# Output projection: drawing the last quarter's sixteen products together and placing the first block's logits, transposes and counts behind them

## The reference

```
h = rmsnorm(x) ;  proj = h @ w_in
merged = sigmoid(g_conv) * y_conv + sigmoid(g_attn) * y_attn
x = x + merged @ w_out                       # the output projection
logits = rmsnorm(x) @ w_router + b_router    # 32 experts
top 4 of 32, gates = softmax of the four
x = x + sum over the four experts of gate * (swiglu(h2 @ w_up[e] + b_up[e]) @ w_down[e] + b_down[e])
```

## Time and profile before

| | |
|---|---|
| three runs | 1146.79, 1147.54, 1148.38 us, median 1147.54 |
| the profiled execution: span from the first to the last instruction | 1145.4 us |
| its own time outside the span | not given by the profile; the median of the runs is 2.1 us over the span |
| PE busy | 1097.6 us (96% of the span) |
| DVE, ACT, POOL busy | 437.5, 188.0, 88.4 us |
| DMA | 444.36 MB, 388 GB/s over the span |
| mean granted TensorE clock | 0.993 |

### The profile page before, as it was taken

How to read it: one execution, slowest core, us unless ns; L and a number is a source line. 1 busy time by engine, 2 the same in 40 slices (tenths; PEclk the granted TensorE clock), 3 DMA queues, 4 the chain that set the end, 5 groups by cost and what they waited for, 6 DMA issues and landing times.

```text
span 1145.4 us, 15065 instructions
## 1 busy us (share of the span) xinstructions
PE 1097.6 (96%) x6055; PEld 497.1 (43%) x6055; DVE 437.5 (38%) x858; ACT 188.0 (16%) x398; POOL 88.4 (8%) x161
## 2 busy tenths in 40 slices
PE   9999999999999999999898999999999999999997
PEld 6689898543333333333333333333333333333332
DVE  4577786753433223233223232323232323232322
ACT  2133341221321101010101010101010101010101
POOL 1785215000000000000000000000000000000000
PEclk9999999999999999999999999999999999999999
DMA  9947629999999999999999999999999999999997
GB/s 313 314 128 186 210 85 353 416 357 425 400 420 426 419 432 431 430 433 431 433 433 429 434 430 433 435 428 434 429 434 431 431 434 429 435 429 434 425 423 287
DMA packets 53206, 444.36 MB, mean 388 GB/s; under 512 B 13101, under 2 KB 19373, under 8 KB 35741
## 3 DMA queue, kind: packets, MB, share of 16 engines
q1 hardware_dynamic: 46712, 435.83, 91.7%
q0 software_dynamic: 5600, 7.32, 2.4%
q10 hardware_dynamic: 852, 0.64, 0.2%
HBM read 439.78 MB, written 2.37 MB: 386 GB/s over the span
## 4 chain that ended last, share of the span: by engine, by line
PE 62%; DMA 37%; DVE 0%; issue 0%; ACT 0%; ACTq 0%; SPq 0%; DVEq 0%
PE pA L2051 32%; PE pB L2051 21%; DMA ring<-in_w_up 21%; DMA ring<-in_w_down 10%; PE pM L2051 6%; DMA area<-in_w_up 5%; PE pM L2054 1%; PE pA L2054 1%; DMA x<-in_x_prompt 1%; ACT area L1269 0%; DVE x L1898 0%; SPq L800 0%; DVE conv_row L1812 0%; DVE area L1973 0%; DVE x L1978 0%
## 5 line engine op out<-in xcount | busy, mean ns | idle before, releaser
L2051 PE MATMUL pA<-ring,hn 128*64 128x512 f32 x1536 | 352.6, 602 | 23.0 <-DMA ring<-in_w_up 23.0
L2051 PEld LDWEIGHTS pA<-ring,hn 128*64 128x64 f32 x1536 | 105.3, 137 | 218.8 <-issue 185.5
L2051 PE MATMUL pB<-ring,area 128*64 128x512 f32 (+2 forms) x784 | 171.5, 591 | 6.6 <-DMA ring<-in_w_down 5.8
L2051 PE MATMUL pA<-area,hn 128*64 128x512 f32 x512 | 119.3, 610 | 10.4 <-DMA area<-in_w_up 10.4
L2051 PE MATMUL pB<-area,ring 128*128 128x132 f32 (+2 forms) x928 | 126.4, 327 | 0.0
L2051 PEld LDWEIGHTS pB<-area,ring 128*128 128x128 f32 (+1 forms) x928 | 106.7, 175 | 18.2 <-issue 2.3
L2051 PEld LDWEIGHTS pB<-ring,area 128*64 128x64 f32 (+2 forms) x784 | 58.5, 136 | 101.2 <-issue 87.8
L1898 DVE TENSOR_TENSOR x<-pM,x 128x512 f32<-128x512 f32 x60 | 40.1, 691 | 147.7 <-PE pM L2051 147.7
L1257 ACT ACTIVATE area<-area 128x512 f32<-128x512 f32 x30 | 18.9, 631 | 385.2 <-DVE area L1881 385.2
L1812 DVE COPY conv_row<-pM 128x512 f32<-128x512 f32 x30 | 20.6, 686 | 146.0 <-PE pM L2051 146.0
L2051 PEld LDWEIGHTS pA<-area,hn 128*64 128x64 f32 x512 | 36.2, 139 | 74.5 <-issue 59.7
(11 more groups left out here) (348 smaller groups left out, 907.1 us busy)
## 6 DMA issues: line engine op xcount, KB each, us to landing
ring<-in_w_up SPq DMA_DIRECT2D x36, 4096.0 KB, 29.8
ring<-in_w_down SPq DMA_DIRECT2D x18, 4096.0 KB, 29.0
area<-in_w_up SPq DMA_DIRECT2D x12, 4096.0 KB, 30.2
ring<-in_w_up SPq DMA_DIRECT2D x16, 2048.0 KB, 13.4
area<-in_w_down SPq DMA_DIRECT2D x6, 4096.0 KB, 30.0
ring<-in_w_in SPq DMA_DIRECT2D x22, 1024.0 KB, 10.0
ring<-in_w_down SPq DMA_DIRECT2D x16, 1024.0 KB, 11.6
ring<-in_w_up SPq DMA_DIRECT2D x16, 1024.0 KB, 8.4
```

Of the source, the lines that this page charges most:

```text
L2051: return pe.matmul(out, w, m, start=start, stop=stop, skip_group_check=True)
```

## The change

Only the list is changed. Before, the products of the last quarter were dealt out between the first block's steps; after, the eight of half 0 are drawn in a row behind `rms 0`, and half 1's in six and two with `logits 0` between. `x_cols 3`, `x_cols 4` and `count 0` follow behind all of them, directly ahead of `ahead 1`. `groups 0` moves behind half 0. No instruction is added or removed.

```diff
-          ("s_split", 0), ("out", (1, 0)), ("x_cols", 2), ("rms", 0), ("part", (0, 0, 6)), ("groups", 0), ("x_cols", 3),
-          ("logits", 0), ("part", (0, 6, KT)), ("half", 0), ("part", (1, 0, 4)), ("count", 0), ("part", (1, 4, 6)),
-          ("x_cols", 4), ("part", (1, 6, KT)), ("half", 1), ("ahead", 1), ("x_cols", 5), ("rms", 1), ("logits", 1),
-          ("gather", 1), ("count", 1), ("gather", 2)]
+          ("s_split", 0), ("out", (1, 0)), ("x_cols", 2), ("rms", 0), ("part", (0, 0, KT)), ("half", 0), ("groups", 0),
+          ("part", (1, 0, 6)), ("logits", 0), ("part", (1, 6, KT)), ("half", 1), ("x_cols", 3), ("x_cols", 4), ("count", 0),
+          ("ahead", 1), ("x_cols", 5), ("rms", 1), ("logits", 1), ("gather", 1), ("count", 1), ("gather", 2)]
```

## The result

| | changed kernel | kernel before |
|---|---|---|
| median of 7 runs each (lowest to highest) | 1152.43 us (1148.97 to 1154.76) | 1147.53 us (1146.79 to 1148.44) |
| ratio, 95% interval | 1.0036 [1.0024, 1.0048] | |
| profiled execution: own time, span | 1153.12, 1151.2 us | span 1145.4 us |

The change made the kernel slower by 4.9 us, outside the range of 1147.3 to 1151.0. The span of the profiled execution grew by 5.8 us. Three delays make it up, and only two of them have to do with the change.

The account below looks back on a forecast made before the run. The stream of expert weights was taken as the bound (DMA share 0.99 from 260 us). Waits add +1.7 us to the 1145.4 span, giving 1147.1; with 2.1 kept to the median, 1149.2 us, range 1147.3 to 1151.0.

Parts of the forecast that it names:

- The waits: PE ahead of `count 0` and `ahead 1`: waiting for DVE delays `ahead 1` and so `up(0)` by 1.7 us.
- the first wait: PE behind `x_cols 4`, ahead of `count 0`: stands until DVE has copied `x_cols 3`, about 1.4 us.
- the bounds of 1.45 to 2.3: Range in us for the 1.7 us step: lower from DVE overlaps, upper from a later chain start and loss at `x_cols 5`.
- a cover of 0.2: Last four records of `logits 1`: DVE's copy of `x_cols 5` ends at 236.06, PE arrives at 236.25; no cost taken.
- the 3.05 us: PE at `logits 0`: begins 3.05 us later, said to have 20 more records ahead of it and `x_cols 3` no longer.
- That it carries to the end: From `up(0)` on: refill and every later row move by the same 1.7 us, as the weight stream has no slack.
- The rival in which the delay is absorbed: Expert stage: stream slack or PE's stock of loaded chunks hides the delay, 1147.5 us; chance 9%.
- The gain: Half 1's last product ends 1.1 us earlier and `ahead 1` and `logits 1` follow: 1146.4 us; chance 5%.
- The clock: PE between 232.25 and 234.45 us: clock falls to half rate in the new wait, together +3.4, 1150.9 us; chance 14%.
- nearer the first: Against the clock's fall: the new wait resembles a 1.29 us wait after which sixteen products still took 3.65 us.
- broken by the count: Against the clock's fall: a short count splits PE's standing into 1.4 us and some 0.5 more.
- The section of the Trainium skill that the prediction weighed: "HAM oscillation": waits between groups of matmuls bring back half rate, the next group starts cold; sum 1.7 + 1.7 us.

Follow-up runs that it names:

- wait_only: Kernel before in its own order, with DVE copying `x_cols 4` five times instead of once so that `ahead 1` waits; 1152.57 us, ratio 1.0036.
- two kernels with the fivefold copy: Kernel before with DVE's copy of `x_cols 4` made five times, without and with four spare products ahead of `ahead 1`; 1152.57 and 1150.07 us.
- after_filled2: Second run of the changed kernel with four spare products, three ahead of `count 0` and one ahead of `ahead 1`; 1150.01 us, ratio 1.0024.
- wait_among_products: Kernel before with PE made to wait for the samples' mask ahead of block 1's first output-projection half; 1151.03 us, ratio 1.0039.
- count_late: Kernel before with only `count 0` moved, behind half 1 and directly ahead of `ahead 1`; 1148.74 us, ratio 1.0006.
- after_again: The changed kernel, unchanged, run a second time; 1150.71 us, ratio 1.0030 against the kernel before.
- count_filled: Kernel before with `count 0` moved behind half 1, plus one spare product ahead of `ahead 1`; 1148.05 us, ratio 1.0007.
- logits_early: Changed kernel with `groups 0` moved forward behind six of half 0's products and `logits 0` behind half 0; 1150.10 us, ratio 1.0019.
- three pairs of variants: logits_early, count_late and wait_only, each without and with spare products in its waits; 1150.10 and 1148.93, 1148.74 and 1148.05, 1152.57 and 1150.07 us.

## Why the prediction was wrong

**The waits: right.** From half 0's first product the forecast puts `logits 0` at 230.35 - 223.45 = 6.90 us, it came at 6.82; the first wait was to be 1.4 us and was 1.24; `ahead 1` at 11.00, it came at 10.75; the half of chunk 6 at 4.63, it was issued at 4.58. Without a fall of the clock `up(0)` came 1.58 us later, where 1.7 was forecast, within the bounds of 1.45 to 2.3. The two errors in it have opposite signs. `ahead 1` came 0.25 us sooner than forecast, in three small pieces: `logits 0` 0.08 sooner, DVE 0.07 sooner at it (233.74 - 233.39 = 0.35, not 0.42), and the copy of `x_cols 3` began 0.08 before the addition ahead of it ended (235.80, not 235.47 + 0.41). The way from `ahead 1` to `up(0)`, taken as unchanged, grew by 0.12: the twelve records of `logits 1` took 1.58 us, not 1.42, at the place where the prediction counted on a cover of 0.2. Two slips in the working changed nothing: 16 records and not 20 move ahead of `logits 0` (the 3.05 us are 16 records less `x_cols 3`), and at 234 to 236 us the stream moves 287 GB/s at a DMA share of 0.99, so its engines did not stand idle there.

**That it carries to the end: right.** The rest behind `up(0)` is 903.6 to 905.9 us in all 14 profiles, while the excess goes from 0 to 4.58, and it does not get shorter as the excess grows. The rival in which the delay is absorbed is refuted; wait_only, which leaves the order as it was, pays at the end. (The two kernels with the fivefold copy have the longest rest, 905.8 and 905.9; where their 1.6 us over before lie was not found.) What the clock costs inside the expert stage is absorbed, however. Behind a fall sixteen products take 1.7 us longer, and yet the next long wait ends 58.30 us later (736.47 to 794.77), as it does without a fall (58.29, 678.18 to 736.47), because the shorter waits between shrink. With four falls there (before) PE's waits of 0.3 us and more add up to 38.4 us, with one (after_filled2) to 43.8; three falls fewer are worth 5.1 us, and still the rest is 904.9 there and 904.2 in before. The gain failed as the prediction said it would: half 1's last product ends 8.07 us after half 0's first (9.29 before, by the same rows), but `ahead 1` waits for the count's read.

**The clock: the step that failed.** The sum has nothing for the clock; the prediction gave this rival 14%, because two of three waits of that length in the expert stage had left the clock at 1.00, and because the new wait was "nearer the first" and "broken by the count". In the whole of before's expert stage the wait of 1.29 us is no exception: none of the five waits of 1.29 and 1.30 us was followed by a fall, and four of the nine of 1.85 to 1.87 were, more than the three rows suggest. But both reasons were wrong for this stage. Behind the waits of the expert stage come sixteen products of 512 columns; here come transposes, a count of 0.41 us and small groups. Whether this is the difference that decides was tried once and not settled (wait_among_products); that the waits of the one stage were no measure for the other is plain. In six profiles with PE standing here, for 0.37 to 1.84 us, the clock fell in five; in the five with spare products in the waits and in the two of the kernel before it stayed at 1.00. Five of six against none of five is a split that chance alone would give once in 77; no single pair of profiles would show it. The count, far from breaking the wait, makes a second of it, and in count_late the second alone was followed by a fall. The price was taken as one group at half rate, 1.7 us; measured it is 1.0 and 2.5 in the changed kernel and 1.5 to 3.7 in the variants, since whatever steps stand ahead of `up(0)` while the clock is down run at half rate, and not only the last group.

By the Trainium skill, "TensorE: Matmul & The Clock Gate", section "A second HAM failure mode: psum-queue depth-cycling", frequent short idles of PE between groups of matmuls, as another kernel went round its banks, sent the clock back and forth. The trace of count_late agrees in part: one idle of 0.37 us at a handover of a bank was followed by 0.50, but it is one idle, and the Trainium skill tells of a series. The section of the Trainium skill that the prediction weighed has waits for transfers as its case, each longer than some 2 us of products.

**What the sum would have been.** 1.6 us by the waits and, in two of three profiles, 1.0 or 2.5 by the clock. The three sets of the changed kernel lie 4.9, 3.0 and 4.1 above the kernel before; their pooled median, 1151.81 us, lies 3.9 above its 1147.9. The waits and the 1.6 us that spare products give back make 3.2 of these. The remaining 0.7 stays open: with spare products the kernel should stand at 1147.9 + 1.6 = 1149.5, and stands at 1150.2. Open is also why the clock did not fall in after_again, whose waits are the same to 0.01 us. The distance from the span to the own time, kept at 2.1 us, is 1.75 to 1.96 in every run on record, too little to matter here. No version beat the kernel before; the nearest, count_filled, measures the same as it.

## What to carry to other kernels

Independent products laid between the steps of a handover do two things: they hide the other engine's chain, and they keep PE's clock up; a reordering that gathers them in one place loses both, and the second can cost more than the first. The risk of a wait isn't read from waits of the same length in another stage of the trace; products that nobody needs, put into it, are a cheap test of what the clock costs there. A fall of the clock costs time only where nothing behind it gives way: ahead of `up(0)` it was paid in full, in the expert stage, where PE waits for weights anyway, not at all. Before explaining a difference of a few microseconds between two profiles, run the old and the new kernel once more: here 3.1 of the 5.8 us were chance.

## What was not expected of the hardware

A wait of 0.37 us amid small instructions was followed by a granted clock of 0.50 (count_late), and one pair of 0.56 and 0.37 us by 0.50 in every window from 236 to 244 us (logits_early), although PE was busy for all of the 8 us; behind the 460 waits of 0.3 to 1.3 us in the expert stage it never fell. Products whose result is never read made the way to `up(0)` shorter by 1.5, 3.0 and 3.7 us in the three pairs of variants, with one profile to a side.
